# Third dilation on its own 128 keys, rows raised and lowered in halves

## The chip, the cores and the metric

One core of a Trainium2 chip (trn2). The time is device microseconds of one execution, from a run on the chip; several runs give the median. Matrix products run on TensorE (PE), whose weight loads are listed as PEld; VectorE (DVE), ScalarE (ACT) and GpSimd (POOL) work element by element; SyncE (SP) issues most transfers.

## The reference

One encoder layer over 2048 tokens of width 1024, then a mixture of experts. The change touches the attention alone:

```python
DIL_PAIRS = ((128, 1), (512, 4), (2048, 16))
for g, (w, d) in enumerate(DIL_PAIRS):
    o, l = band_attention(to_strided(q[:, :, sl], d), to_strided(k[:, :, sl], d),
                          to_strided(v[:, :, sl], d), w // (2 * d), DIL_BLOCK)
```

`band_attention` lets query i see keys j with |i - j| <= 64 of its own strided sequence. With dilation 16 such a sequence has 2048 / 16 = 128 tokens, so all keys that a query can see lie in one tile of 128. With dilations 1 and 4 they reach 64 tokens into the tiles beside it. A second attention, with a sliding window of 128 tokens on both sides, has eight query heads and two key heads.

## The kernel before

The stages follow one another: modulation and normalisation (to 86 us), attention with its projection (to about 1165 us), gates and branches, output projection with routing, experts, last norm.

Attention goes in **steps** T = 0 to 127 and three more. Step T handles a tile of 128 tokens. Each of the groups g = 0, 1, 2 (dilations 1, 4, 16) and 3 (sliding window) has 32 tiles: 16 tiles of tokens, twice, two heads (in the window four) a time. The work is pipelined over tiles:

- `raise_tile` (L924, ACT) copies the 128x1024 rows of tile T + 1 to a rounded high part `h_hi`; `lower_tile` (L790, POOL) takes the difference from the rows as low part `h_lo`. Both read `hT` with a step of the dilation and write one of two buffers.
- `project` on PE multiplies eight blocks k of 128, three products each (high by high, high by low, low by high), 384 columns wide: 24 products a step.
- `take_projection` (L991, ACT) evicts q and k to `qk_raw` and v to `v_dil`. For a dilated group v is stored shifted by 64 rows, so that two neighbouring rows of `v_dil` hold the 256 keys of a tile.
- `rotary` (DVE, L1373 to L1377) rotates q and k; PE transposes them (L1853, L1854); DVE copies them to `qst` and `kT_dil` (L1416 to L1419).
- For tile T - 2 PE computes scores against 256 keys (L1884), DVE adds the mask (L1441), takes the maximum (L1446) and negates it (L1452), ACT takes exponentials (L1030).
- For tile T - 3 PE transposes the probabilities (L1870), ACT copies them to `eT` (L1021), PE multiplies with v (L1903), DVE copies the result out (L1465), SP sends it away.

The order of PE in a step is written out: products k = 0 to 3, the transposes of q and k, products 4 and 5, probability transposes (T - 3), scores (T - 2), products 6 and 7, values (T - 3). ACT's order: raise tile T + 1, raise a piece of the next weights (L933), eT of T - 3, take projection T, exponentials of T - 2. POOL's: lower tile T + 1, lower a piece of weights (L799). DVE's: rotary T - 1, its copies, one addition to a sum of late modulation weights (L1389 and L1387, in steps 0 to 63 alone; every eighth step PE has one product for it), mask and maximum of T - 2, output of T - 3.

Groups 0 and 1 are written out step by step. Of group 2 steps 68 to 93 and of group 3 steps 100 to 125 are loops with two steps a turn, whose addresses and semaphore counts are computed in registers. PE waits once a step for the lowered tile, ahead of product 0.

Of the kernel before, what the change touches and what calls it, by code (L numbers as in the profile page):

```python
# [13 lines left out]
ds = bass.ds  # L14
# [102 lines left out]
def body(nc, A, out, ctx):  # L117
# [641 lines left out]
    def _(pool):  # L759
# [12 lines left out]
        for m, w, var in ((mask_dil, HD, 4), (mask_swa, P, 3)):  # L772
# [3 lines left out]
            for v in range(var):  # L776
# [144 lines left out]
    def _(act):  # L921
        act.wait_ge(sem("c_in"), 16)
        nc.scalar.activation(c_sil[:], c_col[:], ACT.Silu).then_inc(sem("c_silu"), 1)
        def raise_tile(T, c, g):  # L924
            tok = first_token(g, tile_of(T))
            nc.scalar.activation(h_hi[c][:], hT[:, :, ds(tok, P, step=dilation(g))], ACT.Copy).then_inc(sem("h_hi_ready"), 1)  # L926

# [362 lines left out]
    def _(dve):  # L1290
# [113 lines left out]
        def step(T, c, gs, loads):  # L1404
# [23 lines left out]
            for u in (0, 1):  # L1428
                if g2 is not None and u in units(g2):
                    S = T - 2  # L1430
                    n = unit(g2, S, u)
                    dve.wait_ge(sem("s_done"), n + 1)
                    w = 256 if g2 < 3 else 384
                    e = e_sb[u][:, :, 0:w]
                    if g2 < 3:
                        src = S_ps[:, 0, :].rearrange("p (h w) -> p h w", h=2)
                        mk = mask_dil
                    else:
                        src, mk = S_ps[:, :, 0:384], mask_swa
                    m = mk[:, ds(mask_index(g2, tile_of(S)), 1), :].broadcast_to([P, 2, w])  # L1440
                    nc.vector.tensor_tensor(e, src, m, ALU.add).then_inc(sem("masked"), 1)  # L1441
# [345 lines left out]
    def _(pe):  # L1787
# [49 lines left out]
        def step(T, c, gs, loads):  # L1837
            g, g1, g2, g3 = gs[1], gs[2], gs[3], gs[4]
            if g is not None:
                pe.wait_ge(sem("h_lo_ready"), T + 1)  # L1840
                pe.wait_ge(sem("w_lo_ready"), TT * (T // TT) + TT)
                wait(pe, sem("proj_evicted"), T - 1)
                project(T, c, g, (0, 1, 2, 3))
# [5 lines left out]
            if g1 is not None:  # L1849
# [9 lines left out]
                last.then_inc(sem("qkT_done"), 1)  # L1859
            if g is not None:  # L1860
                project(T, c, g, (4, 5))
            two = (g2 == 3 or g3 == 3)
            for u in (0, 1):
                if g3 is not None and u in units(g3):
                    n = unit(g3, T - 3, u)
                    pe.wait_ge(sem("exp_done"), n + 1)
                    for h in range(2):
                        for j in range(2 if g3 < 3 else 3):
                            dst = E_ps[:, 0, (2 * h + j) * P:(2 * h + j + 1) * P] if g3 < 3 else E_ps[:, h, j * P:(j + 1) * P]
                            last = nc.tensor.transpose(dst, e_sb[u][:, h, j * P:(j + 1) * P], ident[:])  # L1870
                    last.then_inc(sem("eT_done"), 1)
                if g2 is not None and u in units(g2):
# [20 lines left out]
                if g3 is not None and u in units(g3):  # L1893
# [242 lines left out]
```

## Time and profile before

| | us |
|---|---|
| median of 3 runs | 3007.15 |
| lowest, highest | 2998.29, 3008.34 |
| the profiled execution | 3004.46 |
| its span | 3002.7 |

| engine | busy us of the span | share |
|---|---|---|
| PE | 2676.9 | 89% |
| PEld | 2311.5 | 77% |
| DVE | 1838.8 | 61% |
| ACT | 1503.6 | 50% |
| POOL | 868.4 | 29% |

Busy shares are over all stages. In the attention the timeline repeats itself step by step, so that one step, and the distance between the same operation in two steps, tell nearly all of a group. A line of the timeline has the start in us from the start of the span, the duration in us, engine, line, operation, what is written and read, and, where the engine sat idle before, for how long and what ended it. A matrix product of plain fp32 shows as two records. Weight loads show when PE comes to a product.

### The profile page before, as it was taken

To read this page: it belongs to the slowest core of one execution; us is meant where nothing else is said; L and a number is where in the kernel's file an instruction comes from. 1 tells how busy PE (TensorE), PEld (TensorE's weight loads), DVE (VectorE), ACT (ScalarE), POOL (GpSimd) and SP (SyncE) were. 2 spreads that over 40 slices of the span, in tenths; PEclk is the share of its full clock that TensorE was granted. 3 is DMA by queue.
4 is the path that set the end of the run, shared out by engine and by line. 5 is a ranking of instruction groups with operands and counts; after the bars stand their busy time and mean duration, and the time that the engine had idled before them with its cause. 6 is when DMAs were issued, how large, how long until landed. Compare 5 with 4: busy or idle time off the path is not lost.

```text
span 3002.7 us, 47236 instructions
## 1 busy us (share of the span) xinstructions
PE 2676.9 (89%) x14033; PEld 2311.5 (77%) x14035; DVE 1838.8 (61%) x3121; ACT 1503.6 (50%) x2613; POOL 868.4 (29%) x615
## 2 busy tenths in 40 slices
PE   3899999999999996899999699749999999999950
PEld 3899888999888885788888588638788888888740
DVE  6688788666677675545441244467866635375858
ACT  5555666666445443434442222226756634375754
POOL 5544555555222211344434111101211111111110
PEclk8999999999999997999999899869999999999985
DMA  6122222000000002444433443428977846486988
GB/s 246 56 63 67 59 58 59 28 25 26 20 18 15 10 11 82 138 132 132 139 113 116 138 168 140 154 102 330 385 284 288 314 147 224 140 314 251 378 318 326
DMA packets 191339, 451.53 MB, mean 150 GB/s; under 512 B 36366, under 2 KB 86582, under 8 KB 189196
## 3 DMA queue, kind: packets, MB, share of 16 engines
q1 hardware_dynamic: 172236, 389.46, 37.1%
q0 software_dynamic: 14400, 52.44, 4.7%
q10 hardware_dynamic: 4608, 8.39, 0.7%
q8 instruction: 56, 0.92, 0.1%
q14 instruction: 39, 0.32, 0.0%
HBM read 380.01 MB, written 70.21 MB: 150 GB/s over the span
## 4 chain that ended last, share of the span: by engine, by line
PE 65%; DVE 11%; issue 9%; DMA 7%; ACT 4%; POOL 2%; DVEq 0%; SPq 0%; ACTq 0%; POOLq 0%
PE bank L2053 13%; PE bank L1833 12%; PE bank L1937 6%; PE bank L1981 4%; DMA sb_w_in<-in_w_gate_up 4%; PE S_ps L2064 3%; PE E_ps L2064 3%; PE O_ps L1903 3%; PE S_ps L1937 3%; PE E_ps L1937 3%; PE S_ps L1886 3%; PE S_ps L1884 2%; PE E_ps L1870 2%; PE S_ps L1981 1%; POOL sb_h_lo L792 1%
## 5 line engine op out<-in xcount | busy, mean ns | idle before, releaser
L792 POOL TENSOR_TENSOR sb_h_lo<-sb_hT,sb_h_hi 128x1024 fp32r<-128x1024 f32 x128 | 339.4, 2652 | 602.8 <-ACT sb_h_hi L926 602.8
L2053 PE MATMUL bank<-sb_gu,sb_x_hiT 128*128 (+1 forms) x1568 | 495.3, 397 | 12.2 <-DVE sb_x_loT L1693 9.5
L1833 PE MATMUL bank<-sb_w_hi,sb_h_hi 128*128 128x384 f32 (+1 forms) x1024 | 403.2, 394 | 11.0 <-POOL sb_h_lo L792 8.8
L2053 PEld LDWEIGHTS bank<-sb_gu,sb_x_hiT 128*128 128x128 f32 x1568 | 294.1, 190 | 75.1 <-issue 11.8
L1833 PE MATMUL bank<-sb_w_hi,sb_h_lo 128*128 128x384 f32 (+1 forms) x1024 | 345.6, 338 | 0.0
L1833 PE MATMUL bank<-sb_w_lo,sb_h_hi 128*128 128x384 f32 (+1 forms) x1024 | 344.9, 337 | 0.0
L1679 DVE TENSOR_TENSOR sb_gu<-sb_w_in,sb_gu 128x1024 f32 (+1 forms) x256 | 301.2, 1221 | 64.8 <-ACT sb_gu L1180 62.9
L1180 ACT ACTIVATE sb_gu<-sb_w_in 128x1024 f32 (+1 forms) x256 | 257.0, 1059 | 109.5 <-DMA sb_w_in<-in_w_gate_up 88.5
L850 POOL TENSOR_TENSOR sb_g_lo<-sb_g_raw,sb_g_hi 128x1408 fp32r<-128x1408 f32 x64 | 212.4, 3339 | 342.0 <-ACT sb_g_hi L1055 342.0
L2053 PE MATMUL bank<-sb_gu,sb_x_loT 128*128 (+1 forms) x784 | 308.2, 393 | 0.0
L1030 ACT ACTIVATE sb_e_sb<-sb_e_sb,sb_o_row 128x256 f32<-128x256 f32 (+1 forms) x320 | 173.7, 545 | 85.1 <-DVE sb_snk L1457 58.3
L1833 PEld LDWEIGHTS bank<-sb_w_hi,sb_h_hi 128*128 128x128 f32 x1024 | 194.1, 190 | 24.8 <-issue 8.1
L1021 ACT ACTIVATE sb_eT<-E_ps 128x512 f32<-128x512 f32 (+1 forms) x160 | 108.4, 678 | 200.4 <-PE E_ps L1870 199.0
L1833 PEld LDWEIGHTS bank<-sb_w_lo,sb_h_hi 128*128 128x128 f32 x1024 | 194.6, 190 | 10.4
L926 ACT ACTIVATE sb_h_hi<-sb_hT 128x1024 fp32r<-128x1024 f32 (+1 forms) x128 | 195.7, 1529 | 5.8 <-POOL sb_v_swa L835 5.7
L1833 PEld LDWEIGHTS bank<-sb_w_hi,sb_h_lo 128*128 128x128 f32 x1024 | 193.0, 188 | 0.0
L2053 PEld LDWEIGHTS bank<-sb_gu,sb_x_loT 128*128 128x128 f32 x784 | 148.1, 189 | 33.4
L890 POOL COPY sb_gi<-sb_gather_idx 128x1 int32 (+1 forms) x51 | 14.4, 282 | 495.8 <-PE S_ps L2043 429.7
L1688 DVE TENSOR_TENSOR sb_dn_lo<-sb_w_in,sb_dn_hi 128x1024 fp32r<-128x1024 f32 x128 | 150.2, 1220 | 8.1 <-ACT sb_dn_hi L1194 7.1
L1194 ACT ACTIVATE sb_dn_hi<-sb_w_in 128x1024 fp32r<-128x1024 f32 x128 | 130.3, 1067 | 16.7 <-DMA sb_w_in<-in_w_expert_down 16.3
L900 POOL DMA_INDIRECT y_d<-sb_y_sb,sb_si x49 | 56.3, 1150 | 276.0 <-ACT sb_y_sb L1209 276.0
L998 ACT ACTIVATE sb_qk_raw<-bank 128x256 f32<-128x256 f32 (+1 forms) x128 | 50.8, 397 | 169.1 <-PE bank L1833 169.1
(371 smaller groups left out, 6215.0 us busy)
## 6 DMA issues: line engine op xcount, KB each, us to landing
sb_w_in<-in_w_gate_up SPq DMA_DIRECT2D x256, 512.0 KB, 6.4
sb_w_in<-in_w_expert_down SPq DMA_DIRECT2D x128, 512.0 KB, 5.4
sb_g_raw<-in_w_gb SPq DMA_DIRECT2D x64, 704.0 KB, 4.0
sb_late_w<-in_w_ada SPq DMA_DIRECT2D x64, 256.0 KB, 2.9
sb_yp<-y_d SPq DMA_DIRECT2D x16, 1024.0 KB, 6.9
sb_w_raw<-in_w_qkv SPq DMA_DIRECT2D x112, 96.0 KB, 2.0
sb_x_round<-in_x SPq DMA_DIRECT2D x4, 2048.0 KB, 9.4
sb_wada<-in_w_ada SPq DMA_DIRECT2D x8, 1024.0 KB, 5.0
```

The source lines that it names most:

```text
L792: nc.gpsimd.tensor_tensor(h_lo[c][:], tile_src(g, T), h_hi[c][:].bitcast(F32), ALU.subtract).then_inc(sem("h_lo_ready"), 1)
L850: nc.gpsimd.tensor_tensor(g_lo[c][:, cols], g_raw[j][:], g_hi[c][:, cols].bitcast(F32), ALU.subtract).then_inc(sem("g_lo_ready"), 1)
L926: nc.scalar.activation(h_hi[c][:], hT[:, :, ds(tok, P, step=dilation(g))], ACT.Copy).then_inc(sem("h_hi_ready"), 1)
L1030: last = nc.scalar.activation(e_sb[u][:, h, 0:w], e_sb[u][:, h, 0:w], ACT.Exp, bias=row[:, h, HD:HD + 1], scale=SCALE, accum_out=row[:, h, ...
L1180: nc.scalar.activation(gu[:, ds(gu_row(e, 0, k), 1), :], w_in[slot][:].rearrange("p (a n) -> p a n", a=1), ACT.Copy).then_inc(sem("gu_hi_r ...
L1679: nc.vector.tensor_tensor(gu[:, ds(gu_row(e, 1, k), 1), :], raw, gu[:, ds(gu_row(e, 0, k), 1), :].bitcast(F32), ALU.subtract).then_inc(sem ...
L1688: nc.vector.tensor_tensor(dn_lo[:, k, :], w_in[(KD + k) % RING][:], dn_hi[:, k, :].bitcast(F32), ALU.subtract).then_inc(sem("dn_lo_ready"), 1)
L1833: last = nc.tensor.matmul(bank[c][:, 0:PASS_COLS].rearrange("p (a m) -> p a m", a=1), x[c][:, k, :], w[:, ds(row + k, 1), :], start=(k == ...
L1937: nc.tensor.matmul(PS[4 * c + j][:].rearrange("p (a n) -> p a n", a=1), w[:, col:col + P], x[:, k:k + 1, :], start=(k == 0 and a == 0), st ...
L1981: last = nc.tensor.matmul(PS[2 * c + j][:], x[c][:, k, :], w[:, k, j * 512:(j + 1) * 512], start=(k == 0 and a == 0), stop=(k == KD - 1 an ...
L2053: last = nc.tensor.matmul(PS[j][:].rearrange("p (a n) -> p a n", a=1), x[:, k, :], gu[:, ds(gu_row(e, part, k), 1), j * DE:(j + 1) * DE], ...
L2064: last = nc.tensor.matmul(PS[4 + j][:], x[:, k, :], w[:, k, j * 512:(j + 1) * 512], start=(k == 0 and a == 0), stop=(k == KE - 1 and a == 2))
```

## The change

For group 2 the keys are the tile's own 128: v is stored unshifted by one copy in the place of two, the scores are 128 columns wide and read the tile's keys (at an offset of 64 in `kT_dil`), the mask is its middle 128 columns, exponentials and `eT` are 128 wide, two probability transposes go in the place of four, and two value products in the place of four. In all groups raise and lower work in two halves of four blocks each, each with its own semaphore count, and PE waits for the first half ahead of product 0, for the second ahead of product 4.

```diff
+    KEYS = (256, 256, P, 384)
+    HALVES = (slice(0, KD // 2), slice(KD // 2, KD))
+
+    def tile_src(g, T, ks):
+        tok = first_token(g, tile_of(T))
+        return hT[:, ks, ds(tok, P, step=dilation(g))]
...
         def lower_tile(T, c, g):
-            pool.wait_ge(sem("h_hi_ready"), T + 1)
-            nc.gpsimd.tensor_tensor(h_lo[c][:], tile_src(g, T), h_hi[c][:].bitcast(F32), ALU.subtract).then_inc(sem("h_lo_ready"), 1)
+            for j, ks in enumerate(HALVES):
+                pool.wait_ge(sem("h_hi_ready"), 2 * T + j + 1)
+                nc.gpsimd.tensor_tensor(h_lo[c][:, ks], tile_src(g, T, ks), h_hi[c][:, ks].bitcast(F32), ALU.subtract).then_inc(sem("h_lo_ready"), 1)
...
         def raise_tile(T, c, g):
-            tok = first_token(g, tile_of(T))
-            nc.scalar.activation(h_hi[c][:], hT[:, :, ds(tok, P, step=dilation(g))], ACT.Copy).then_inc(sem("h_hi_ready"), 1)
+            for ks in HALVES:
+                nc.scalar.activation(h_hi[c][:, ks], tile_src(g, T, ks), ACT.Copy).then_inc(sem("h_hi_ready"), 1)
 ...
-            if g < 3:
+            if g == 2:
+                last = nc.scalar.activation(v_dil[:, ds(t, 1), :], src[:, 256:384].rearrange("p (a m) -> p a m", a=1), ACT.Copy)
+            elif g < 3:
 ...
-                w = 256 if g3 < 3 else 384
-                src = E_ps[:, 0, :] if g3 < 3 else E_ps[:, :, 0:384]
+                w = KEYS[g3]
+                src = E_ps[:, 0, 0:2 * w] if g3 < 3 else E_ps[:, :, 0:384]
...
-                    m = mk[:, ds(mask_index(g2, tile_of(S)), 1), :].broadcast_to([P, 2, w])
+                    keys = slice(HD, HD + w) if g2 == 2 else slice(0, w)
+                    m = mk[:, ds(mask_index(g2, tile_of(S)), 1), keys].broadcast_to([P, 2, w])
 ...
-                pe.wait_ge(sem("h_lo_ready"), T + 1)
+                pe.wait_ge(sem("h_lo_ready"), 2 * T + 1)
                 project(T, c, g, (0, 1, 2, 3))
...
             if g is not None:
+                pe.wait_ge(sem("h_lo_ready"), 2 * T + 2)
                 project(T, c, g, (4, 5))
...
-                        for j in range(2 if g3 < 3 else 3):
+                        nj = KEYS[g3] // P
+                        for j in range(nj):
...
-                            last = nc.tensor.matmul(S_ps[:, 0, h * 256:(h + 1) * 256], qst[c][:, h, :], kT_dil[:, ds(t * P, 256)], start=True, stop=True)
+                            last = nc.tensor.matmul(S_ps[:, 0, h * w:(h + 1) * w], qst[c][:, h, :], kT_dil[:, ds(t * P + (HD if g2 == 2 else 0), w)], start=True, stop=True)
...
-                    nj = 2 if g3 < 3 else 3
+                    nj = KEYS[g3] // P
```

## Rows read from the trace of the kernel before

**Rows 1.** Busy time by stretch, columns in its header

```profile
core 0: us, PE busy (x) PEld busy (x) DVE busy (x) ACT busy (x) POOL busy (x), PEclk, DMA share, GB/s
...
300.00:548.00 248.00, 236.24 (x1434) 218.50 (x1432) 200.15 (x411) 163.57 (x342) 128.25 (x69) 1.00 0.20 57
...
548.00:750.00 202.00, 201.71 (x1265) 194.99 (x1264) 124.34 (x334) 139.53 (x300) 103.25 (x61) 1.00 0.09 25
```

**Rows 2.** Waits of attention: engine, line, waited for: us, times, longest

```profile
PE S_ps L1886 <- DVE sb_kT_swa L1422: 24.6, 29, 1.2
...
PEld bank L1853 <- DVE sb_qk_rot L1377: 16.3, 22, 1.4
...
PE bank L1833 <- POOL sb_h_lo L792: 8.8, 5, 7.1
```

**Rows 3.** Timeline, weight loads in a third-dilation step: start us, us, what

```profile
602.12 0.53 PEld L1870 LDWEIGHTS E_ps<-sb_ident,sb_e_sb 128*128 128x128 f32 x4
...
602.61 0.73 PEld L1884 LDWEIGHTS S_ps<-sb_kT_dil,sb_qst 128*128 128x128 f32 x4
...
603.37 0.19 PEld L1833 LDWEIGHTS bank<-sb_w_hi,sb_h_hi 128*128 128x128 f32 x1
...
604.46 1.03 PEld L1903 LDWEIGHTS O_ps<-sb_v_dil,sb_eT 128*128 128x128 f32 x8
...
605.53 0.19 PEld L1833 LDWEIGHTS bank<-sb_w_hi,sb_h_hi 128*128 128x128 f32 x1
```

**Rows 4.** Timeline, the other engines in the same steps

```profile
599.99 1.99 ACT L926 ACTIVATE sb_h_hi<-sb_hT 128x1024 fp32r x1
...
601.88 0.35 ACT L933 ACTIVATE sb_w_hi<-sb_w_raw 128x192 f32 x1
...
602.04 0.29 DVE L1419 COPY sb_kT_dil<-bank 128x128 f32 x1
...
602.20 2.90 POOL L792 TENSOR_TENSOR sb_h_lo<-sb_hT,sb_h_hi 128x1024 fp32r<-128x1024 f32 x1 [3.28 <-ACT sb_h_hi L926]
...
604.83 0.38 ACT L998 ACTIVATE sb_qk_raw<-bank 128x256 f32<-128x256 f32 x1 [1.31 <-PE bank L1833]
...
605.05 0.59 POOL L799 TENSOR_TENSOR sb_w_lo<-sb_w_raw,sb_w_hi 128x192 f32 x1
...
605.24 0.44 DVE L1452 TENSOR_SCALAR sb_o_row<-sb_mx 128x2 f32<-128x2 f32 x1
...
607.18 0.43 DVE L1377 TENSOR_TENSOR sb_qk_rot<-sb_qk_rot,sb_qk_tmp 128x256 f32<-128x256 f32 x1
```

**Rows 5.** Timeline of POOL, lowering of a tile in groups 0, 1, 2

```profile
211.43 2.38 POOL L792 TENSOR_TENSOR sb_h_lo<-sb_hT,sb_h_hi 128x1024 fp32r<-128x1024 f32 x1 [4.16 <-ACT sb_h_hi L926]
...
265.48 2.38 POOL L792 TENSOR_TENSOR sb_h_lo<-sb_hT,sb_h_hi 128x1024 fp32r<-128x1024 f32 x1 [4.13 <-ACT sb_h_hi L926]
...
314.19 2.89 POOL L792 TENSOR_TENSOR sb_h_lo<-sb_hT,sb_h_hi 128x1024 fp32r<-128x1024 f32 x1 [4.22 <-ACT sb_h_hi L926]
...
547.35 2.88 POOL L792 TENSOR_TENSOR sb_h_lo<-sb_hT,sb_h_hi 128x1024 fp32r<-128x1024 f32 x1 [2.66 <-ACT sb_h_hi L926]
...
568.57 2.88 POOL L792 TENSOR_TENSOR sb_h_lo<-sb_hT,sb_h_hi 128x1024 fp32r<-128x1024 f32 x1 [3.34 <-ACT sb_h_hi L926]
```

**Rows 6.** Timeline, two steps of group 1, with the late addition

```profile
512.21 0.74 DVE L1389 SCALAR_TENSOR_TENSOR sb_late_sum<-sb_late_w,sb_c_sil,sb_late_sum 128x512 f32<-128x512 f32 x1
...
518.87 2.89 POOL L792 TENSOR_TENSOR sb_h_lo<-sb_hT,sb_h_hi 128x1024 fp32r<-128x1024 f32 x1 [2.62 <-ACT sb_h_hi L926]
...
519.19 3.12 DVE L1389 SCALAR_TENSOR_TENSOR sb_late_sum<-sb_late_w,sb_c_sil,sb_late_sum 128x512 f32<-128x512 f32 x1
...
526.97 3.06 POOL L792 TENSOR_TENSOR sb_h_lo<-sb_hT,sb_h_hi 128x1024 fp32r<-128x1024 f32 x1 [4.21 <-ACT sb_h_hi L926]
```

**Rows 7.** Timeline, looped sliding-window step: key copy, then the scores

```profile
1011.84 0.28 DVE L1422 COPY sb_kT_swa<-bank 64x128 f32 x1
...
1012.41 0.94 PEld L1886 LDWEIGHTS S_ps<-sb_kT_swa,sb_qst 128*128 128x128 f32 x4 [1.38 <-issue]
```

More of the change, by code:

```diff
@@ L785, in _ @@
                     ch.join()
-        def tile_src(g, T):
-            tok = first_token(g, tile_of(T))
-            return hT[:, :, ds(tok, P, step=dilation(g))]
         def lower_tile(T, c, g):
-            pool.wait_ge(sem("h_hi_ready"), T + 1)
-            nc.gpsimd.tensor_tensor(h_lo[c][:], tile_src(g, T), h_hi[c][:].bitcast(F32), ALU.subtract).then_inc(sem("h_lo_ready"), 1)
+            for j, ks in enumerate(HALVES):
+                pool.wait_ge(sem("h_hi_ready"), 2 * T + j + 1)
+                nc.gpsimd.tensor_tensor(h_lo[c][:, ks], tile_src(g, T, ks), h_hi[c][:, ks].bitcast(F32), ALU.subtract).then_inc(sem("h_lo_ready"), 1)
         def lower_piece(n, c):
@@ L924, in raise_tile @@
         def raise_tile(T, c, g):
-            tok = first_token(g, tile_of(T))
-            nc.scalar.activation(h_hi[c][:], hT[:, :, ds(tok, P, step=dilation(g))], ACT.Copy).then_inc(sem("h_hi_ready"), 1)
+            for ks in HALVES:
+                nc.scalar.activation(h_hi[c][:, ks], tile_src(g, T, ks), ACT.Copy).then_inc(sem("h_hi_ready"), 1)
         def raise_piece(T, c):
@@ L1026, in exponentials @@
                 act.wait_ge(sem("max_ready"), n + 1)
-                w = 256 if g2 < 3 else 384
+                w = KEYS[g2]
                 row = o_row[c][u]
@@ L1432, in step @@
                     dve.wait_ge(sem("s_done"), n + 1)
-                    w = 256 if g2 < 3 else 384
+                    w = KEYS[g2]
                     e = e_sb[u][:, :, 0:w]
                     if g2 < 3:
-                        src = S_ps[:, 0, :].rearrange("p (h w) -> p h w", h=2)
+                        src = S_ps[:, 0, 0:2 * w].rearrange("p (h w) -> p h w", h=2)
                         mk = mask_dil
@@ L1867, in step @@
                     for h in range(2):
-                        for j in range(2 if g3 < 3 else 3):
-                            dst = E_ps[:, 0, (2 * h + j) * P:(2 * h + j + 1) * P] if g3 < 3 else E_ps[:, h, j * P:(j + 1) * P]
+                        nj = KEYS[g3] // P
+                        for j in range(nj):
+                            dst = E_ps[:, 0, (nj * h + j) * P:(nj * h + j + 1) * P] if g3 < 3 else E_ps[:, h, j * P:(j + 1) * P]
                             last = nc.tensor.transpose(dst, e_sb[u][:, h, j * P:(j + 1) * P], ident[:])
@@ L1880, in step @@
                     wait(pe, sem("masked"), n)
-                    t = tile_of(S)
+                    t, w = tile_of(S), KEYS[g2]
                     for h in range(2):
                         if g2 < 3:
-                            last = nc.tensor.matmul(S_ps[:, 0, h * 256:(h + 1) * 256], qst[c][:, h, :], kT_dil[:, ds(t * P, 256)], start=True, stop=True)
+                            last = nc.tensor.matmul(S_ps[:, 0, h * w:(h + 1) * w], qst[c][:, h, :], kT_dil[:, ds(t * P + (HD if g2 == 2 else 0), w)], start=True, stop=True)
                         else:
```

## Prediction

> **What bounds the kernel now.** I read the table of stretches first. Only the attention stretch is touched, about 86 to 1165 us. In the third dilation TensorE (PE) is busy 201.71 of 202.00 us at the full clock, in the second dilation 236.24 of 248.00 us [rows 1]. So in the third dilation work taken from PE is time, provided that nothing else is nearly as late; in the second something already holds PE up. The list of waits shows PE held by rotated rows (16.3 us), by the window's key copies (24.6 us), and by POOL's lowering only 8.8 us, 7.1 of it one wait at the start [rows 2]. The timeline then gives the margins.
>
> A step of the third dilation takes (602.20 - 568.57) / 5 = 6.73 us, five tiles apart [rows 4, 5]. Call p the moment at which ScalarE (ACT) takes a finished projection (604.83). One step earlier p was 598.10; ACT raised the next tile from 599.99 to 601.98, p + 1.9 to p + 3.9, POOL lowered it from 602.20 to 605.10, p + 4.1 to p + 7.0, and PE's weight load for that step came at 605.53, p + 7.4 [rows 3, 4]. **The margin of raise and lower is 0.4 us.** It is the ring that the first edit alone would run into.
>
> **Group 1 is slower than PE needs.** Eight steps of group 0 take 265.48 - 211.43 = 54.05 us, 6.76 each with one late product in eight; 32 steps of group 1 take 547.35 - 314.19 = 233.16 us, 7.29 each, with the same PE work [rows 5]. In rows 6 the late addition, 0.74 us alone, starts 0.32 us behind a lowering and lasts 3.12 us: it ends at 522.31, 0.55 us after POOL's 521.76. The two don't run together; VectorE (DVE) waits for the whole POOL operation. Mask, maximum and exponentials stand behind it, then ACT's raise, then POOL again, 8.10 us after the last time (518.87 to 526.97) [rows 6]. A short step follows, in which the addition (512.21, 0.74) comes ahead of POOL.
>
> The Trainium skill ("SBUF — State Buffer", Who interferes with whom) says that a DVE instruction with two SBUF inputs fully blocks against a GpSimd one that reads SBUF, whichever starts first. The 3.12 us agree. By that rule the rotations, too, can be caught by POOL once the steps are shorter; that is the last rival.
>
> **The change, part by part.**
>
> 1. Less PE work in the third dilation. Weight loads mark the order: four probability transposes take 602.61 - 602.12 = 0.49 us, four score passes of 256 columns 603.37 - 602.61 = 0.76, eight value passes 605.53 - 604.46 = 1.07 [rows 3]. Two transposes and four value passes go: 0.25 + 0.53. The four score passes stay, with 128 columns: no saving at one end, half (0.38) at the other; I take the transposes' 0.12 us a pass, also 128 columns wide, so 0.49 and 0.27 saved. Sum 1.05 us a step (0.78 to 1.16), 32 steps: 33.6 us (25 to 37).
>
> 2. What is late next there. (a) Key copies to scores. The copies end at 602.33, p + 4.2; scores follow at 602.61 [rows 3, 4]. With 0.25 us fewer transposes PE could be there at 602.36, 0.03 behind the copies. In a looped window step, where PE does wait, 0.29 us lie between copy (1012.12) and load (1012.41) [rows 7]. So up to 0.26 us a step comes back, nothing at the other end; I take 0.2 in the 26 looped steps: 5 us. (b) Rotation to transposes. Rows of the next step are rotated by 607.61, p + 2.8. PV work shortened by 0.53 brings PE to the transposes that much sooner, but the rotation also starts sooner: it follows the O copy, which follows PV, and the second V copy before it is gone. I cost it at nothing; if its start didn't move, 0.5 us a step. (c) Scores' mask, maximum and exponentials work on half the columns and become earlier, not later; ACT's eT copy is halved and stands 1 us before its use.
>
> 3. Halves. A whole raise is 1.99 us for 1024 elements and a 192-element one 0.35; a half at that slope is 1.0 [rows 4]. POOL: 2.90 and 0.59, a half 1.5. So two halves cost ACT some 0.1 and POOL some 0.1 to 0.2 us more than one whole, beside PE's work. In the third dilation, after part 1: projection taken p to p + 0.7, exponentials to p + 1.5 (they were p + 0.9 to 1.9), first half raised p + 2.5, lowered p + 4.2, second half lowered p + 5.7. The new p is p + 5.7, PE asks for the first half 0.5 us after it (p + 6.2), and for the second after twelve more products and two transposes, over 2 us later. Margins 2.0 and 2.7 us. Unsplit, the lowering would end at 1.5 + 2.0 + 0.2 + 2.9 = p + 6.6, 0.4 too late. So the halves are what lets part 1 through in full. Queued behind ACT's second half are the weight raise and eT, both with over 0.3 us in hand; behind POOL's is the lowering of weights for the next pass.
>
> 4. Halves in group 1. The late addition comes at p + 4.2 (the copies' end). The whole lowering started at p + 4.1 and blocked it to p + 7.0; now the first half runs p + 3.1 to p + 4.6. The addition gets in between the halves (so it did ahead of the weight lowering at 521.76) and is done by p + 5.3, before the scores it delays are there (about p + 5.6: 1.0 us of products before the next p). POOL's second half ends near p + 6.9 and PE wants it at about p + 9.6. Group 1 then runs at group 0's 6.76: 32 x (7.29 - 6.76) = 17 us.
>
> 5. Extra waits on PE and their register work. Added before products 4 and 5 in 128 steps; behind it are these products, the scores and all who wait for them. It is always satisfied by margin 2.7 us. A looped one needs a computed count: nothing at one end (PE has products in its queue meanwhile), the 0.29 us of rows 7 at the other, where a looped wait stands open. 52 looped steps: 0 to 15 us; I take 1.5, near the lower end, since the array is fed here [rows 7]. Group 0 gains nothing: PE is full. In the sliding window DVE's key copies set the step, and the raise is over long before; nothing.
>
> Sum: -33.6 + 5 - 17 + 1.5 = **-44 us**. The profiled execution took 3004.46 us (span 3002.7), so 2960; the median of the three runs is 2.7 us higher, 3007.15, and gives 2963. I say 2961.
>
> **Rivals.**
> - *The late addition misses the gap.* If it comes after the first half's end it waits for the second. Then the ring is: POOL end, addition 0.6, mask, maximum and negation 1.6, exponentials 1.0, half a raise 1.2, two halves 3.0, sum 7.4 a step, no better than 7.29. For it: a margin of only 0.4 us (p + 4.2 against p + 4.6). Against: a late product moves it only every eighth step. Group 1 gains nothing: 2978.
> - *The third dilation gives half.* Rotation (2b) at 0.5 us a step, or the key wait at its full 0.26 plus scores that save nothing at 128 columns: 16 us lost of 34. 2976.
> - *The edit does little.* PE isn't the limit in either group and another engine takes over at today's step: within 9 us of before. For it: all engines of a step hang on each other; against: 201.71 of 202.00.
> - *Slower: POOL catches the rotation.* The first half of the lowering now starts 1 us earlier in groups 1 and 2 (p + 2.7 to 3.1) and at p + 2.6 in group 0. The last rotation starts at p + 2.35 now (607.18). If a half starts ahead of it in each step, the rotation waits 1.3 to 1.5 us for it, and PE's transposes stand right behind. Half of the 96 steps of groups 0 to 2 caught: 48 x 1.4 = 67 us, less the 44 gained: 3028. From 44 / 1.4 = 31 caught steps on the kernel is slower. It decides at 0.25 us of order in group 0. Against: the rotation starts off the same event p, and isn't behind the exponentials as the raise is.
>
> **How the numbers follow.** Forecast 0.60 at 2961, own range 2950 to 2970. Late addition misses 0.15; third dilation halved 0.14; little change 0.06; slower 0.05. The range takes in the first two rivals: 2950 to 2984. About 0.3% (9 us) is what a measurement can tell from none: faster by more 0.60 + 0.15 + 0.14 and a part of the fourth, 0.91; same 0.05; slower 0.04.
>
> **What would show it.** Steps of the third dilation at 5.6 to 5.9 us between first lowerings; PE busy over 95% there; four records of the value products for eight. Group 1 at 6.8 us a step, the late addition never over 2.2 us, two lowerings of 1.5 us. Group 0 and the window within 0.1 us a step of before. Wrong would be: waits of PE for POOL in the third dilation, a late addition of 3 us, rotations over 0.7 us, or scores of 0.19 us a pass with 128 columns.

## The result, and the profile after

The changed kernel takes 2949.99 us (median of 4 runs, 2947.07 to 2955.52), the kernel before 3003.95 us in the runs beside it (4, 2998.29 to 3008.34). The ratio is 0.9825, 95% interval 0.9809 to 0.9841: 54 us less, where 44 were forecast (46 if the 2961 is set against the 3007.15 known then). The profiled execution took 2950.1 us, of which the span is 2948.4.

The same two stretches as in [rows 1], in the kernel after (columns: PE, PEld, DVE, ACT and POOL busy with instruction counts, granted clock, DMA share, GB/s):

```profile
core 0 of [0], span 2948.4 us
core 0: us, PE busy (x) PEld busy (x) DVE busy (x) ACT busy (x) POOL busy (x), PEclk, DMA share, GB/s
300.00:548.00 248.00, 246.95 (x1551) 234.93 (x1549) 182.96 (x444) 175.11 (x402) 146.86 (x111) 1.00 0.21 59
548.00:750.00 202.00, 198.74 (x1247) 187.83 (x1247) 127.79 (x390) 129.96 (x340) 115.99 (x99) 1.00 0.10 27
```

PE is now full in the first stretch too (246.95 of 248.00 against 236.24). The second reaches into the sliding window, which begins sooner.

The best clock for this kernel is one event per step: ACT's start on a finished projection. These are projections 0, 31, 63, 95 and 127 of 128 in the kernel after, then the same in the kernel before:

```profile
95.17 0.39 ACT L1005 ACTIVATE sb_qk_raw<-bank 128x256 f32<-128x256 f32 x1 [1.58 <-PE bank L1843]
...
301.98 0.38 ACT L1005 ACTIVATE sb_qk_raw<-bank 128x256 f32<-128x256 f32 x1 [1.31 <-PE bank L1843]
...
518.81 0.38 ACT L1005 ACTIVATE sb_qk_raw<-bank 128x256 f32<-128x256 f32 x1 [1.31 <-PE bank L1843]
...
704.98 0.38 ACT L1005 ACTIVATE sb_qk_raw<-bank 128x256 f32<-128x256 f32 x1 [1.12 <-PE bank L1843]
...
1078.22 0.44 ACT L1005 ACTIVATE sb_qk_raw<-bank 128x320 f32<-128x320 f32 x1 [1.01 <-PE bank L1843]
```

```profile
96.58 0.38 ACT L998 ACTIVATE sb_qk_raw<-bank 128x256 f32<-128x256 f32 x1 [3.70 <-PE bank L1833]
...
302.28 0.38 ACT L998 ACTIVATE sb_qk_raw<-bank 128x256 f32<-128x256 f32 x1 [1.31 <-PE bank L1833]
...
536.12 0.38 ACT L998 ACTIVATE sb_qk_raw<-bank 128x256 f32<-128x256 f32 x1 [1.31 <-PE bank L1833]
...
752.76 0.38 ACT L998 ACTIVATE sb_qk_raw<-bank 128x256 f32<-128x256 f32 x1 [1.31 <-PE bank L1833]
...
1128.23 0.44 ACT L998 ACTIVATE sb_qk_raw<-bank 128x320 f32<-128x320 f32 x1 [1.00 <-PE bank L1833]
```

| stretch (steps) | before | after | difference |
|---|---|---|---|
| start, to projection 0 | 96.58 | 95.17 | -1.4 |
| group 0 (31) | 205.70 | 206.81 | +1.1 |
| group 1 (32) | 233.84 | 216.83 | -17.0 |
| group 2 (32) | 216.64 | 186.17 | -30.5 |
| window (32) | 375.47 | 373.24 | -2.2 |
| to projection 127 | 1128.23 | 1078.22 | -50.0 |

So 50.0 of the 54 us lie up to projection 127, where the change is. The other 4 lie behind it (1874.5 us before, 1870.2 after, to the end of the span). From there on code and work are the same, yet this part takes 1864 to 1881 us in the profiled executions of the kernels here that do the same work (l1 below does not), so I don't put a cause to 4 us of it.

A step of the third dilation after, PE's weight loads first, as [rows 3] shows them before (L1882 transposes of probabilities, L1896 scores, L1915 values, L1863 transposes of rotated rows, L1843 products):

```profile
599.93 0.31 PEld L1882 LDWEIGHTS E_ps<-sb_ident,sb_e_sb 128*128 128x128 f32 x2
600.34 0.52 PEld L1896 LDWEIGHTS S_ps<-sb_kT_dil,sb_qst 128*128 128x128 f32 x4
600.78 0.19 PEld L1843 LDWEIGHTS bank<-sb_w_hi,sb_h_hi 128*128 128x128 f32 x1
...
601.79 0.58 PEld L1915 LDWEIGHTS O_ps<-sb_v_dil,sb_eT 128*128 128x128 f32 x4
602.29 0.19 PEld L1843 LDWEIGHTS bank<-sb_w_hi,sb_h_hi 128*128 128x128 f32 x1
...
604.54 0.14 PEld L1863 LDWEIGHTS bank<-sb_ident,sb_qk_rot 128*128 128x128 f32 x1 [0.21 <-DVE sb_qk_rot L1386]
...
608.03 0.19 PEld L1843 LDWEIGHTS bank<-sb_w_hi,sb_h_hi 128*128 128x128 f32 x1
...
610.06 0.14 PEld L1863 LDWEIGHTS bank<-sb_ident,sb_qk_rot 128*128 128x128 f32 x1
...
610.34 0.19 PEld L1843 LDWEIGHTS bank<-sb_w_hi,sb_h_hi 128*128 128x128 f32 x1
```

The other engines in the same step (compare [rows 4]):

```profile
599.86 0.29 DVE L1428 COPY sb_kT_dil<-bank 128x128 f32 x1
...
602.16 0.38 ACT L1005 ACTIVATE sb_qk_raw<-bank 128x256 f32<-128x256 f32 x1 [1.26 <-PE bank L1843]
...
603.37 2.14 ACT L933 ACTIVATE sb_h_hi<-sb_hT 128x512 fp32r x2
...
604.71 3.07 POOL L799 TENSOR_TENSOR sb_h_lo<-sb_hT,sb_h_hi 128x512 fp32r<-128x512 f32 x2 [2.03 <-ACT sb_h_hi L933]
```

Scores last 600.78 - 600.34 = 0.44 us (0.76 before), values 602.29 - 601.79 = 0.50 (1.07). With p = 602.16 the raise begins at p + 1.2 and the first lowering at p + 2.5; both halves end at 607.78, p + 5.6. PE asks for the first half at 608.03 (p + 5.9) and for the second after the transposes, at 610.34 (p + 8.2). The margin of the whole tile was 0.4 us; the second half now has 2.6.

Group 0 pays 1.1 us, and the trace shows where. In its first step ACT has no exponentials to do yet, so the raise starts at once, the first half of the lowering starts 0.30 us ahead of the last rotation (L1386, 0.42 us alone), and the rotation lasts 0.95 us longer:

```profile
96.72 2.81 POOL L799 TENSOR_TENSOR sb_h_lo<-sb_hT,sb_h_hi 128x512 fp32r<-128x512 f32 x2 [0.73 <-ACT sb_h_hi L933]
97.02 1.37 DVE L1386 TENSOR_TENSOR sb_qk_rot<-sb_qk_rot,sb_qk_tmp 128x256 f32<-128x256 f32 x1
98.45 0.14 PEld L1863 LDWEIGHTS bank<-sb_ident,sb_qk_rot 128*128 128x128 f32 x1 [1.55 <-DVE sb_qk_rot L1386]
```

The second step does the same (102.88, again 1.37 us). From projection 0 to 1 and from 1 to 2 it takes 5.86 and 6.91 us, for 4.92 and 5.97 before: 1.9 us lost in two steps, of which the other 29 steps give 0.8 back. In the other 126 steps the last rotation takes its normal time.

### The profile page after: what moved, and what is told of

Same layout as the page of the kernel before. It is cut to its first block, busy times and chain, and to the rows that moved or that the text cites. A ratio compares the mean times of both kernels' runs of the same rounds, so it can differ in the third digit from the quotient of the medians.

```text
span 2948.4 us, 47198 instructions
## 1 busy us (share of the span) xinstructions
PE 2636.8 (89%) x13841; PEld 2279.4 (77%) x13843; DVE 1778.1 (60%) x3121; ACT 1487.0 (50%) x2709; POOL 895.7 (30%) x743
## 4 chain that ended last, share of the span: by engine, by line
PE 72%; DVE 10%; issue 8%; DMA 6%; ACT 3%; POOL 1%; DVEq 0%; SPq 0%; ACTq 0%; POOLq 0%
PE bank L1843 15%; PE bank L2065 14%; PE bank L1949 6%; PE bank L1993 4%; PE S_ps L2076 4%; PE E_ps L2076 3%; PE O_ps L1915 3%; PE S_ps L1949 3%; PE E_ps L1949 3%; DMA sb_w_in<-in_w_gate_up 3%; PE S_ps L1898 3%; PE S_ps L1896 2%; PE E_ps L1882 2%; PE S_ps L1993 2%; PE O_ps L1960 1%
## 5 line engine op out<-in xcount | busy, mean ns | idle before, releaser
L799 POOL TENSOR_TENSOR sb_h_lo<-sb_hT,sb_h_hi 128x512 fp32r<-128x512 f32 x256 | 371.2, 1471 | 528.9 <-ACT sb_h_hi L933 528.9
L1843 PE MATMUL bank<-sb_w_hi,sb_h_hi 128*128 128x384 f32 (+1 forms) x1024 | 398.2, 389 | 5.9 <-POOL sb_h_lo L799 5.4
L1843 PE MATMUL bank<-sb_w_hi,sb_h_lo 128*128 128x384 f32 (+1 forms) x1024 | 344.6, 336 | 0.0
L1843 PE MATMUL bank<-sb_w_lo,sb_h_hi 128*128 128x384 f32 (+1 forms) x1024 | 343.8, 336 | 0.0
L933 ACT ACTIVATE sb_h_hi<-sb_hT 128x512 fp32r<-128x512 f32 (+1 forms) x256 | 209.0, 865 | 5.9 <-POOL sb_v_swa L842 5.8
L1843 PEld LDWEIGHTS bank<-sb_w_hi,sb_h_hi 128*128 128x128 f32 x1024 | 193.9, 189 | 15.9 <-issue 6.3
L1843 PEld LDWEIGHTS bank<-sb_w_lo,sb_h_hi 128*128 128x128 f32 x1024 | 194.3, 190 | 9.6
L1030 ACT ACTIVATE sb_eT<-E_ps 128x512 f32<-128x512 f32 (+2 forms) x160 | 101.6, 635 | 196.5 <-PE E_ps L1882 196.4
L1039 ACT ACTIVATE sb_e_sb<-sb_e_sb,sb_o_row 128x256 f32<-128x256 f32 (+2 forms) x320 | 166.4, 524 | 62.8 <-DVE sb_snk L1467 59.6
L1843 PEld LDWEIGHTS bank<-sb_w_hi,sb_h_lo 128*128 128x128 f32 x1024 | 192.7, 188 | 0.0
L897 POOL COPY sb_gi<-sb_gather_idx 128x1 int32 (+1 forms) x51 | 17.4, 342 | 503.2 <-PE S_ps L2055 434.9
```

What stands on the lines that cost most here:

```text
L799: nc.gpsimd.tensor_tensor(h_lo[c][:, ks], tile_src(g, T, ks), h_hi[c][:, ks].bitcast(F32), ALU.subtract).then_inc(sem("h_lo_ready"), 1)
L933: nc.scalar.activation(h_hi[c][:, ks], tile_src(g, T, ks), ACT.Copy).then_inc(sem("h_hi_ready"), 1)
L1039: last = nc.scalar.activation(e_sb[u][:, h, 0:w], e_sb[u][:, h, 0:w], ACT.Exp, bias=row[:, h, HD:HD + 1], scale=SCALE, accum_out=row[:, h, ...
L1843: last = nc.tensor.matmul(bank[c][:, 0:PASS_COLS].rearrange("p (a m) -> p a m", a=1), x[c][:, k, :], w[:, ds(row + k, 1), :], start=(k == ...
```

## The experiments

"Total" is the median of 4 to 5 runs with its ratio to the kernel before on the same chip. Groups 1 and 2 are the stretches defined above, read from one profiled execution of each kernel.

| kernel | total us | ratio (95%) | group 1 | group 2 | to projection 127 |
|---|---|---|---|---|---|
| before | 3003.95 | | 233.84 | 216.64 | 1128.23 |
| after | 2949.99 | 0.9825 (0.9809 to 0.9841) | 216.83 | 186.17 | 1078.22 |
| k1_keys_only | 2979.68 | 0.9924 (0.9907 to 0.9941) | 234.02 | 200.07 | 1108.72 |
| h1_halves_only | 2979.11 | 0.9914 (0.9897 to 0.9930) | 216.92 | 213.88 | 1108.21 |
| w1_pe_waits_for_both | 2956.28 | 0.9833 (0.9817 to 0.9849) | 216.97 | 188.35 | 1082.65 |
| l2_late_earlier | 2985.28 | 0.9934 (0.9917 to 0.9950) | 218.70 | 216.32 | 1114.44 |
| l1_late_small | 2960.45 | 0.9859 (0.9841 to 0.9876) | 226.57 | 216.22 | 1120.28 |
| r1_raise_whole | 2968.70 | 0.9881 (0.9863 to 0.9898) | 222.62 | 197.63 | 1093.77 |
| r2_raise_whole_pe_both | 2971.79 | 0.9898 (0.9880 to 0.9915) | 226.52 | 201.50 | 1102.63 |
| r3_max_in_psum | 2961.92 | 0.9863 (0.9847 to 0.9879) | 221.70 | 190.26 | 1085.72 |
| u2_all_written_out | 2928.03 | 0.9749 (0.9731 to 0.9766) | 216.92 | 181.62 | 1056.21 |
| u3_all_written_out_max_in_psum | 2926.24 | 0.9739 (0.9725 to 0.9753) | 216.88 | 181.62 | 1056.09 |

**Each part alone.** k1 has the 128 keys, with raise, lowering and PE's wait whole as before:

```diff
-            for ks in HALVES:
-                nc.scalar.activation(h_hi[c][:, ks], tile_src(g, T, ks), ACT.Copy).then_inc(sem("h_hi_ready"), 1)
+            nc.scalar.activation(h_hi[c][:], tile_src(g, T, slice(0, KD)), ACT.Copy).then_inc(sem("h_hi_ready"), 1)
...
-                pe.wait_ge(sem("h_lo_ready"), 2 * T + 2)
                 project(T, c, g, (4, 5))
```

> The narrow keys alone: raise, lower and PE's wait are whole again, as before. My theory (the ring over raise and lower is 0.4 us from the limit before the change): with p the start of the eviction of a finished projection, exponentials end at p + 1.5, the whole raise at p + 3.5, the whole lowering at p + 6.6; PE asks for it 0.5 us after the next p, so a step of the third dilation can't be shorter than about 6.15 us (it is 5.70 in the changed kernel, 6.73 in the kernel before). Of the 30.5 us gained in the third dilation some 16 stay, group 1 stays at 7.3 us a step: about 2988 us, PE waits for the lowering in each step of the third dilation. Rival (the halves are of no use to the third dilation, which PE alone bounds): a step of 5.7 us there, all 30 us of gain, 2974 us.

h1 has the halves, with 256 keys in the third dilation as before:

```diff
-    KEYS = (256, 256, P, 384)
+    KEYS = (256, 256, 256, 384)
```

> The halves alone, keys of the third dilation 256 wide as before. Theory: group 1 falls from 7.3 to 6.76 us a step (234 to 217 us in 32 steps) because the late addition gets in between two lowerings or comes behind a shorter one; third dilation stays at 6.7 us a step; 17 to 19 us gained, about 2986 us. Rival (group 1 gained by something else, for example by the earlier raise alone or by noise): then the late addition would still last 2 to 3 us in many steps, or group 1 stay above 7 us.

Measured: in group 2 the keys alone give 216.64 - 200.07 = 16.6 us, the halves alone 2.8, both together 30.5. So **11 us of the 30.5 exist only in combination**. This rests on the stretches. The totals came out 8 and 7 us lower than expected; they give 24 and 25 us for the parts and 54 for both, a combined effect of 5 us, with some 5 us of uncertainty on each of the three. That neither shows the 11 nor speaks against it. In group 1 the halves give all 17 us (216.92) and the keys nothing (234.02). The reason for the combination stands in the trace of k1, ACT's projection, POOL's lowering of a tile, and PE's first product of the next:

```profile
599.80 0.39 ACT L1003 ACTIVATE sb_qk_raw<-bank 128x256 f32<-128x256 f32 x1 [1.23 <-PE bank L1841]
...
603.24 2.91 POOL L798 TENSOR_TENSOR sb_h_lo<-sb_hT,sb_h_hi 128x1024 fp32r<-128x1024 f32 x1 [2.75 <-ACT sb_h_hi L931]
...
605.52 0.58 PEld L1912 LDWEIGHTS O_ps<-sb_v_dil,sb_eT 128*128 128x128 f32 x4
606.59 0.19 PEld L1841 LDWEIGHTS bank<-sb_w_hi,sb_h_hi 128*128 128x128 f32 x1 [0.49 <-issue]
```

The lowering ends at 606.15, which is p + 6.35 for p = 599.80. Only 0.44 us later, at 606.59, PE loads the first weights of the next tile, after 0.49 us of nothing (23 such gaps between 560 and 700 us, 10.9 us in all). This is the ring of raise and lowering that the forecast expected to end 0.4 us too late, and the profile calls it "issue", not POOL. PE's busy time between 560 and 700 us falls to 132.18 of 140.00; it is 139.45 after.

**Is it the wait by halves?** In w1 everything is as after, but PE waits for both halves ahead of the first product:

```diff
-                pe.wait_ge(sem("h_lo_ready"), 2 * T + 1)
+                pe.wait_ge(sem("h_lo_ready"), 2 * T + 2)
...
-                pe.wait_ge(sem("h_lo_ready"), 2 * T + 2)
                 project(T, c, g, (4, 5))
```

> The changed kernel, but PE waits for both halves ahead of product 0; raise and lower still work in halves. Theory: in the third dilation the second half is lowered at about p + 5.85 and PE asks for it at p + 6.2, in group 1 the margin is larger: no step gets longer by more than 0.05 us, time within 3 us of the changed kernel (2950). Rival (the projection's waiting for each half carries gain of its own): the third dilation at 5.9 us a step or more, 5 us or more lost.

Group 2 takes 188.35 us against 186.17, group 1 the same. So waiting for each half by itself is worth 2.2 us of the 30.5. The total is 6 us longer, more than the 3 us that I allowed, but its interval overlaps that of after. The profiled execution of w1 is 14.8 us longer than that of after, with 2.3 us in the start and 10.4 behind projection 127, where the code is the same: I take the 2.2. It is 0.07 us a step, a little over the 0.05 expected. How it comes about isn't shown: between 560 and 700 us PE is busy 139.64 us, as much as after (139.45). More of the negations of group 2 last over 0.25 us (24 of 32, for 14 after), but nothing here ties the 2.2 us to them.

**Is it the earlier raise?** In r1 ACT raises the tile whole, POOL lowers it in halves behind that, PE waits as after:

```diff
-            for ks in HALVES:
-                nc.scalar.activation(h_hi[c][:, ks], tile_src(g, T, ks), ACT.Copy).then_inc(sem("h_hi_ready"), 1)
+            nc.scalar.activation(h_hi[c][:], tile_src(g, T, slice(0, KD)), ACT.Copy).then_inc(sem("h_hi_ready"), 1)
...
-                pool.wait_ge(sem("h_hi_ready"), 2 * T + j + 1)
+            pool.wait_ge(sem("h_hi_ready"), T + 1)
```

> The changed kernel with ScalarE's raise whole again (one operation); POOL lowers in two halves behind it and PE waits for each half. Theory (the third dilation needs only that the first half be there at about p + 6.2): raise ends p + 3.5, first half lowered p + 5.2, second p + 6.7 against PE's demand at p' + 2.8 = p + 8.5: step of the third dilation 5.7 to 5.9 us, group 1 at 6.6 to 6.9 us a step, within 6 us of the changed kernel (2950). Rival (the earlier raise is what matters, since POOL can't start before it): third dilation over 6.1 us as with the narrow keys alone.

r2 is r1 with PE waiting for both halves, the edit of w1:

> As r1_raise_whole, but PE waits for both halves ahead of product 0. Now neither the earlier raise nor the wait by halves helps: second half lowered at p + 6.7, PE asks at p' + 0.5, so the third dilation's step is at least 6.2 us, as with the narrow keys alone (6.17); about 16 us more than the changed kernel in the third dilation, group 1 between 6.7 and 7.3 us: 2968 to 2985 us. Rival: within 3 us of r1_raise_whole, which would mean that the wait by halves never matters.

**r1 came out slower than I expected:** 6.07 us in a looped step of group 2, 197.63 us for the group, 2968.7 in all, 18.7 more than after for the 6 allowed. Of these, 11.5 us are in group 2 and 5.8 in group 1 (222.62, 6.96 a step); the latter I haven't traced. My expectation looked only at when PE needs the lowered rows, and there r1 had enough time. The trace shows another ring:

```profile
602.74 3.02 POOL L799 TENSOR_TENSOR sb_h_lo<-sb_hT,sb_h_hi 128x512 fp32r<-128x512 f32 x2 [2.50 <-ACT sb_h_hi L932]
...
604.85 0.94 DVE L1461 TENSOR_SCALAR sb_o_row<-sb_mx 128x2 f32<-128x2 f32 x1
...
605.73 0.59 POOL L806 TENSOR_TENSOR sb_w_lo<-sb_w_raw,sb_w_hi 128x192 f32 x1
...
605.82 0.40 ACT L1038 ACTIVATE sb_e_sb<-sb_e_sb,sb_o_row 128x128 f32<-128x128 f32 x1 [0.48 <-DVE sb_o_row L1461]
...
605.90 0.70 DVE L1381 TENSOR_TENSOR sb_qk_rot<-sb_qk_raw,sb_cos_t 128x256 f32<-128x256 f32 x1
...
606.61 1.98 ACT L932 ACTIVATE sb_h_hi<-sb_hT 128x1024 fp32r x1
```

The negation of two columns (L1461) starts at 604.85 and ends at 605.79, with POOL's pair of halves (605.76). It takes 0.17 us when it is alone. Exponentials wait for it, the raise stands behind the exponentials, and the next lowering behind the raise: POOL's end, 0.06 to the exponentials, 0.8 for them, 2.0 for the raise, 0.2 to POOL, 3.0 of lowering make 6.07 us. Besides, the rotation (0.70 for 0.42) is caught by the lowering of the weights, and PE then waits 0.56 us for it (11.2 us in 21 waits between 560 and 700 us). In r2 PE waits for the lowering ahead of that, as in k1, and most looped steps take 6.1 to 6.3 us: 201.50 in all, 226.52 in group 1. In the stretches r2 is 3.9 us longer than r1 in each of the two groups, so the wait by halves does matter when the raise is whole; the totals, 3.1 us apart, can't tell.

**r3 tests that ring.** It is r1, with the row maximum of the dilations in spare PSUM columns:

```diff
-                    nc.vector.tensor_reduce(mx[:], e, AX.X, ALU.max).then_inc(sem("maxed"), 1)
+                    mo = E_ps[:, 1, 508:510] if g2 < 3 else mx[:]
+                    nc.vector.tensor_reduce(mo, e, AX.X, ALU.max).then_inc(sem("maxed"), 1)
...
-                        nc.vector.tensor_scalar(negm, mx[:], -SCALE, None, ALU.mult).then_inc(sem("max_ready"), 1)
+                        nc.vector.tensor_scalar(negm, mo, -SCALE, None, ALU.mult).then_inc(sem("max_ready"), 1)
```

> As r1_raise_whole (raise whole, lowering in halves behind it, 6.07 us a step of the third dilation, 2968.7 us), but in the three dilations the row maximum is written to two spare PSUM columns, and the negation reads it there and not from SBUF. Theory: in r1 the 128x2 negation of 0.17 us starts while POOL lowers and lasts 0.94 us, to POOL's end; exponentials, raise and the next lowering stand behind it, so this is the ring of 6.07 us. With its input in PSUM it isn't blocked: at most 0.35 us, exponentials start with the projection's eviction, about 0.5 us sooner, and a step falls to 5.7 to 5.9 us; the lowering of the weights still catches the rotation by 0.3 us. Total 2957 to 2965, first accumulation wait of the third dilation 6 to 11 us shorter. Rival 1: the negation's output, in SBUF, is what is blocked: 0.9 us and 6.0 to 6.1 us a step still, 2967 to 2971. Rival 2: the negation is freed, but the rotation, caught by POOL, sets the step on its own: negation short, 6.0 us a step.

All 96 negations of r1, and then all of r3 (columns: shortest, median and longest in ns, then first and last start):

```profile
L1461 DVE TENSOR_SCALAR sb_o_row<-sb_mx x96: 168/520/1120, 107.0 to 732.6; 128x2 f32<-128x2 f32 x96
```

```profile
L1462 DVE TENSOR_SCALAR sb_o_row<-E_ps x96: 160/160/164, 107.1 to 724.5; 128x2 f32<-128x2 f32 x96
```

Group 2 falls from 197.63 to 190.26 us (about 5.8 in a looped step), the total to 2961.9, within the forecast. So **the negation behind POOL cost r1 7.4 us**, 7.4 of the 11.5 us that separate r1 from the kernel after in this group. Both rivals fall: no negation is blocked, and the rotation alone doesn't hold the step at 6.0. The 4.1 us still left I only put down to the rotation, untested: in r3 PE waits for it 5.2 us in 18 waits between 560 and 700 us.

**The late addition in group 1.** l2 is the kernel before, where the addition stands behind the rotation and ahead of the copies instead of behind them:

```diff
                 if g1 < 3:
                     rotary(S, g1)
+                if late_piece(T) is not None:
+                    late_add(T)
...
-            if late_piece(T) is not None:
+            if g1 is None and late_piece(T) is not None:
                 late_add(T)
```

> The kernel before with one thing moved: DVE makes the late addition right behind the rotation, ahead of its wait for the transposes, at about p + 2.6 where it is idle, not behind the key copies at p + 4.2. Raise and lower are whole and as late as before. Theory (group 1 is slow only because the late addition starts behind a lowering that starts at p + 4.1 and is blocked for its whole length): group 1 at 6.76 us a step, the addition 0.74 us long in nearly all steps, 17 us gained, about 2987 us. Rival (group 1 is slow because the raise and the lowering of rows with a step of 4 tokens are long in themselves, 2.0 and 2.9 us): no gain, 3004 us.

In l1, also from the kernel before, the addition takes 8 columns of 512. It leaves out the other 504 of the second modulation's sums; the rows then choose other experts (47 blocks for 49), so its total isn't comparable and only the attention is read.

```diff
-                ins = nc.vector.scalar_tensor_tensor(acc, w, by, acc, ALU.mult, ALU.add)
+                ins = nc.vector.scalar_tensor_tensor(late_sum[i % 2][:, 0:8], late_w[m % 2][:, 0:8], by, late_sum[i % 2][:, 0:8], ALU.mult, ALU.add)
```

> The kernel before, with the late addition on 8 columns of 512 in 56 of its 64 steps (the other columns are left out of the sum, so later modulation is not the reference's). Its own work falls from 0.74 to under 0.3 us. Theory (a wait for a whole POOL operation, whatever the size of the addition): it still lasts up to 2.9 us where it starts behind a lowering, and group 1 stays well above group 0's step: 6.9 to 7.2 us a step, at most half of the 17 us gained. Rival (DVE has too much to do in these steps): 6.76 us a step, 17 us gained.

All 56 late additions in the kernel before, in the kernel after, in l2 and in l1:

```profile
L1389 DVE SCALAR_TENSOR_TENSOR sb_late_sum<-sb_late_w,sb_c_sil,sb_late_sum x56: 740/1982/3262, 100.2 to 533.5; 128x512 f32<-128x512 f32 x56
```

```profile
L1398 DVE SCALAR_TENSOR_TENSOR sb_late_sum<-sb_late_w,sb_c_sil,sb_late_sum x56: 743/1129/1608, 99.7 to 516.2; 128x512 f32<-128x512 f32 x56
```

```profile
L1389 DVE SCALAR_TENSOR_TENSOR sb_late_sum<-sb_late_w,sb_c_sil,sb_late_sum x56: 743/744/2869, 98.0 to 518.6; 128x512 f32<-128x512 f32 x56
```

```profile
L1389 DVE SCALAR_TENSOR_TENSOR sb_late_sum<-sb_late_w,sb_c_sil,sb_late_sum x56: 215/1357/2853, 100.7 to 526.1; 128x8 f32<-128x8 f32 x56
```

In l2, with whole raise and lowering, group 1 takes 218.70 us: 15.1 of the 17.0 us can be had by the place of one DVE instruction alone. The addition is over 1 us long only twice, 2.87 and 2.86 us in the first two steps of group 0, which takes 2.5 us more than before. In l1 an addition of 8 columns (0.22 us alone) still lasts up to 2.85 us. It is the wait for POOL's operation that costs, not the addition's work; shrinking it gives back 7.3 us, moving it out of POOL's way twice that.

**Written out.** In the kernels so far groups 0 and 1 are written out, while 26 of the 32 steps of group 2 and 24 of the window's run in loops (I had counted 26 there, too). In u2 the changed kernel has all of them written out:

```diff
-            for T in range(T0, end if g < 2 else T0 + 4):
+            for T in range(T0, end if g < 4 else T0 + 4):
                 straight(T)
-            if g < 2:
+            if g < 4:
```

> The changed kernel with the steps of the third dilation and of the sliding window written out, no loops in the attention. Theory (open waits of a looped step are followed by register work before the next product: 0.19 to 0.29 us against 0.06): third dilation from 5.70 to 5.53 us a step as its written-out steps now, the window from 12.27 to about 11.7 us: 26 x 0.17 + 26 x 0.6 = 20 us less, 2930 us. Rival (the two loads at once of the weights or instruction fetch make the written-out steps as slow as the looped ones): no change, 2950 us.

u3 is u2 with the maximum in PSUM, the edit of r3:

> As u2_all_written_out (the changed kernel with all steps of the third dilation and the window written out, 2928.0 us), with the same maximum in PSUM. Theory: with the raise in halves the negation is hardly ever caught (median 0.17 us, longest 0.66), so nothing changes: 5.5 us a step, 2925 to 2931. Rival: in the first and second dilation, too, the negation waits for POOL now and then, and some us come off: 2918 to 2924.

u2 beats both kernels: 2928.0 us. Group 2 gains 4.6 us (5.53 a looped step for 5.70), the window 17.4, 22 together where 20 were expected. Key copy and the first score load behind it in a window step, in the kernel after and in u2:

```profile
1011.23 0.28 DVE L1431 COPY sb_kT_swa<-bank 64x128 f32 x1
...
1011.81 0.94 PEld L1898 LDWEIGHTS S_ps<-sb_kT_swa,sb_qst 128*128 128x128 f32 x4 [1.38 <-issue]
```

```profile
1003.80 0.28 DVE L1431 COPY sb_kT_swa<-bank 64x128 f32<-64x128 f32 x1
...
1004.13 0.94 PEld L1898 LDWEIGHTS S_ps<-sb_kT_swa,sb_qst 128*128 128x128 f32 x4 [0.48 <-DVE sb_kT_swa L1431]
```

From the copy's end to the load it is 1011.81 - 1011.51 = 0.30 us in the loop and 1004.13 - 1004.08 = 0.05 written out. u3 leaves both groups as they were (181.62 and 216.88); its total, 2926.2, can't be told from u2's. With the raise in halves the negation costs nothing that can be seen: in u2 it is over 0.25 us in 7 of 96 cases, in the kernel after in 18 (longest 0.585), with PE busy 139.45 of 140.00 us all the same.

## Why the prediction was right, step by step

**1. Less PE work, right.** Forecast 1.05 us a step: transposes 0.25, values 0.53, scores 0.27. A written-out step went from 6.59 to 5.52 us, 1.07 less: values 1.07 - 0.50 = 0.57, scores 0.76 - 0.44 = 0.32, the rest, 0.2, transposes. Scores of 128 columns do take 0.11 us a pass, as the transposes' row had it [rows 3]; the fear of 0.19 was empty.

**2a. Key copies to scores, too dear.** I took 5 us. After, the copy ends at 600.15 and the load comes at 600.34, and from the two transposes to the scores it takes 0.41 us for the 0.28 of u2 (603.85 to 604.13 there): about 0.13 us a step. But a looped step fell from 6.73 to 5.70, 1.03 less, nearly as much as a written-out one. So only 0.04 x 26 = 1 us of the 5 is a new cost: a looped step was 6.73 - 6.59 = 0.14 us longer than a written-out one before the change, too. **This is the term that was mis-sized**, by 4 us. The scores and values of the group's last tiles still run in the window's first steps, so group 2 and window together, -32.7, are what stands against -33.6 + 5 = -28.6.

**2b. Rotation, right to cost it near nothing.** It is late by 0.21 us in every second looped step (604.54 above), 0.1 on average; written out not at all.

**3. The margins, right as numbers, but the reason was only half of it.** Forecast: second half lowered at p + 5.7, margins 2.0 and 2.7; measured p + 5.6 and, with the first half over by about p + 4.1, 1.8 and 2.6. Unsplit, 0.4 us too late: k1 shows 0.49 us of gap a step and 6.25 us on average. "The halves are what lets part 1 through in full" is shown by k1 and h1. But I argued only with the time at which PE needs the rows. r1 satisfies that and still loses 11.5 us in group 2. The other half is that a lowering that starts earlier also **ends before DVE's negation**: in the step shown it ends at 607.78, and the negation starts at 607.95.

**4. Group 1, right to 0.1 us.** -17.0 as forecast, 6.78 us a step for 6.76, the addition never over 1.61 us. l2 shows the mechanism on its own. In the profile after, of one such step:

```profile
495.49 3.52 POOL L799 TENSOR_TENSOR sb_h_lo<-sb_hT,sb_h_hi 128x512 fp32r<-128x512 f32 x2 [2.52 <-ACT sb_h_hi L933]
...
496.47 1.13 DVE L1398 SCALAR_TENSOR_TENSOR sb_late_sum<-sb_late_w,sb_c_sil,sb_late_sum 128x512 f32<-128x512 f32 x1
```

With p = 492.47 the addition comes at p + 4.0 (forecast 4.2) and the lowering at p + 3.0 (forecast 3.1). It waits 0.4 us for the first half, runs its 0.74, and the pair of halves stretches from 3.06 to 3.52: it got in between.

**5. Extra waits, near the lower end.** 1.5 us forecast. w1, without the second wait, is nowhere shorter by more than 0.3 us: group 0 206.87 us, group 1 216.97, window 373.00, against 206.81, 216.83 and 373.24. It is nothing that these traces can show; in group 2, where w1 loses 2.2 us by waiting early, the wait's own cost can't be told apart. (There are 50 looped steps, not the 52 of the sum.)

**The rivals.** The late addition didn't miss the gap. The third dilation didn't give half, and another engine didn't take over; both would have needed a ring at today's step, and k1 (54% of the gain in group 2) is how that looks. *POOL catches the rotation* did happen in the changed kernel, in 2 of the 96 steps where 31 would have eaten the gain: the last rotation of the first two steps of group 0 lasts 1.37 us, over the 0.7 that I had named as a sign of being wrong. The forecast's "group 0 gains nothing" left this out; it is 1.9 us of loss, seen in all kernels with raise and lowering both in halves (group 0 at 206.8 to 206.9 us; the kernel before, k1, l1, r1 and r2 have 204.9 to 205.7). From the third step on the exponentials hold the raise back, and POOL starts behind the rotation. In r1 POOL catches the first rotation (0.70 us), yet there it isn't the larger cost. I had the mechanism right, but missed its most costly victim, the negation. The page I had drawn on, the Trainium skill ("SBUF — State Buffer", Who interferes with whom), names besides the two-input instructions a second kind that contends with GpSimd, tensor_scalar in its 2-port mode; and "VectorE: DVE Perf Modes" (Mode 2×_2P) says that this mode needs its operands in SBUF. r1 and r3 agree with both: 0.17 us becomes up to 1.12 with the input in SBUF, and is 0.16 in all 96 cases with it in PSUM.

**The total.** The sum was -44, the attention gave -50.0. Of the 6 us between them, 5.6 lie in group 2 and window (-32.7 against -28.6 + 1.5): 4 of step 2a, 1.5 of step 5 and 0.6 of step 1 make 6.1, so 0.5 us is unaccounted for. The start (-1.4) and group 0 (+1.1) nearly cancel. Another 4 us lie in later stages, where no term of the forecast is. They take the time to the very edge of the range, 2949.99 us for a lower end of 2950. The mechanisms held, but that the total didn't fall clear of the range is luck.

## What to carry to other kernels

When an edit shortens the bounding engine's step, write down the margin of every ring in that step first: here one of 0.4 us would have taken 11 of 30 us, and splitting a producer kept them. Look at the first steps of a pipeline by themselves, where an engine has less to do and starts sooner. For each DVE instruction that a GpSimd operation can hold up ask not only "is it early enough for its reader" but also "what does it stand beside": the place of one 0.74 us instruction was worth 15 us, the placement of two columns of data 7. And where waits on the bounding engine stand open in a loop, try the loop written out: here it was worth 22 us.

## What the runs showed that I had not expected

- A 128x2 negation that starts beside a GpSimd operation lasts until that ends: median 0.52 us, longest 1.12, for 0.17 (r1). With its input in PSUM: 0.160 to 0.164 in 96 of 96 (r3).
- The length of a blocked DVE instruction has little to do with its own size: 8 columns up to 2.85 us (l1), 512 columns up to 3.26 (before).
- Between two GpSimd operations issued back to back a waiting DVE instruction is served first; splitting one operation in two thus bounds the wait at half (1.61 us for 3.26 at most, the addition's own 0.74 included), for 0.1 to 0.2 us more of POOL's time, 0.6 where the DVE instruction gets in between.
- An open wait of PE costs 0.30 us in a looped step and 0.05 written out. In the window that is more than one wait's worth: 17.4 us over 24 looped steps, 0.7 each. What the rest of it is wasn't traced.
- The pipeline's first two steps lost 1.9 us to a rotation caught by the lowering, and no later one did.
